# Attention scores of a differential attention layer: one fp32 matmul per score block becomes three fp32r matmuls of rounded parts and rests over 64 rows, with the buffers of the stage laid out anew

## What is computed

```
q = rms_norm((rms_norm(x, ln_g) @ q_w).reshape(b, s, 8, 2, 64), q_norm_g)     # two halves of 64 per head
k = rms_norm(kv[..., :K_DIM].reshape(b, s, 8, 2, 64), k_norm_g)
logits = einsum('bqhcd,bkhcd->bhcqk', qblk, k) * scale + bias               # one per half c, over 64 numbers
p = softmax(where(dist >= 0, logits, -inf))
attn = p[:, :, 0] - lam * p[:, :, 1]
o = rms_norm(einsum('bhqk,bkhd->bqhd', attn, v), subln_g) * (1.0 - lam_init)
mix = o.reshape(b, s, V_TOTAL) @ out_w
```

## Time and profile before

| | |
|---|---|
| median of 3 runs | 2407.59 us (2406.8 to 2408.47) |
| the profiled execution | 2408.69 us, its span 2406.9 us |
| PE / DVE / ACT / POOL busy | 2378.8 / 1408.0 / 1052.7 / 369.7 us |
| differential attention heads, 787 to 985 us of the span | 198 us: PE 194.99, DVE 146.98, ACT 142.42, POOL 18.17 us busy |
| granted TensorE clock | 0.998 of full speed |

### The profile page before, as it was taken

How to read it: one execution, slowest core, us unless ns; L and a number is a source line. 1 busy time by engine, 2 the same in 40 slices (tenths; PEclk the granted TensorE clock), 3 DMA queues, 4 the chain that set the end, 5 groups by cost and what they waited for, 6 DMA issues and landing times.

```text
span 2406.9 us, 29799 instructions
## 1 busy us (share of the span) xinstructions
PE 2378.8 (99%) x11622; PEld 1933.8 (80%) x11622; DVE 1408.0 (59%) x2204; ACT 1052.7 (44%) x1805; POOL 369.7 (15%) x296
## 2 busy tenths in 40 slices
PE   8999999999999999999999999999999999999998
PEld 6677778888888877788888877787788887888887
DVE  6878776763666778766456557534565445443342
ACT  6654554442444677644234334324443334322223
POOL 0352252210111001121012100001211001110101
PEclk9999999999999999999999999999999999999999
DMA  4542223223223221232332332231243322223322
GB/s 164 105 97 79 79 66 101 97 86 107 97 82 119 80 71 52 72 105 92 99 101 89 99 130 71 79 101 62 66 131 128 113 97 88 89 94 103 101 82 85
DMA packets 74269, 226.21 MB, mean 94 GB/s; under 512 B 8080, under 2 KB 12304, under 8 KB 74000
## 3 DMA queue, kind: packets, MB, share of 16 engines
q1 hardware_dynamic: 69696, 215.90, 27.7%
q10 hardware_dynamic: 4432, 8.39, 2.0%
HBM read 215.87 MB, written 8.39 MB: 93 GB/s over the span
## 4 chain that ended last, share of the span: by engine, by line
PE 61%; DVE 1%; issue 0%; ACT 0%; POOL 0%; POOLq 0%; DVEq 0%
PE bank L1162 60%; PE bank L1166 1%; DVE t L2030 0%; DVE t L2027 0%; DVE t L2038 0%; ACT t L1562 0%; DVE t L2034 0%; POOL t L2597 0%; ACT t L1565 0%; POOLq L2816 0%; DVE t L2520 0%; DVEq L2816 0%; DVE t L2366 0%; DVE t L2526 0%; DVEq L771 0%
## 5 line engine op out<-in xcount | busy, mean ns | idle before, releaser
L1162 PE MATMUL bank<-t 128*128 128x512 f32 (+6 forms) x11196 | 2354.7, 376 | 18.4 <-DVE t L2030 8.7
L1162 PEld LDWEIGHTS bank<-t 128*128 128x128 f32 (+2 forms) x11196 | 1890.6, 185 | 451.5 <-issue 80.1
L1562 ACT ACTIVATE t<-t 128x1024 fp32r<-128x1024 f32 (+6 forms) x633 | 539.1, 862 | 636.7 <-PE bank L1162 275.3
L2027 DVE TENSOR_TENSOR t<-t 128x1024 fp32r<-128x1024 f32 (+6 forms) x686 | 625.7, 922 | 260.8 <-ACT t L1562 254.7
L1565 ACT ACTIVATE t<-t 128x512 f32<-128x512 f32 (+6 forms) x609 | 367.1, 617 | 460.5 <-DVE t L2027 304.0
L2597 POOL TENSOR_TENSOR t<-t 128x512 f32<-128x512 f32 (+4 forms) x216 | 328.9, 1528 | 1547.5 <-ACT t L1565 558.9
L2027 DVE TENSOR_TENSOR t<-bank,t 128x512 f32<-128x512 f32 (+4 forms) x411 | 276.1, 676 | 454.7 <-PE bank L1162 444.3
L2030 DVE SCALAR_TENSOR_TENSOR t<-t 128x512 f32<-128x512 f32 (+5 forms) x496 | 367.9, 751 | 103.2 <-ACT t L1565 63.0
L1562 ACT ACTIVATE t<-bank 128x512 f32<-128x512 f32 (+4 forms) x151 | 72.2, 498 | 167.1 <-PE bank L1166 145.2
L2600 POOL TENSOR_SCALAR t<-t 128x128 f32<-128x128 f32 (+3 forms) x64 | 40.1, 633 | 477.9 <-ACT t L1562 246.1
L2030 DVE SCALAR_TENSOR_TENSOR t<-bank,t 128x512 f32<-128x512 f32 x56 | 38.5, 688 | 68.9 <-PE bank L1162 68.9
(11 more groups left out here) (29 smaller groups left out, 42.9 us busy)
## 6 DMA issues: line engine op xcount, KB each, us to landing
t<-in_w SPq DMA_DIRECT2D x304, 512.0 KB, 3.3
t<-in_w SPq DMA_DIRECT2D x48, 384.0 KB, 3.0
t<-in_w SPq DMA_DIRECT2D x56, 320.0 KB, 2.9
t<-in_w SPq DMA_DIRECT2D x28, 256.0 KB, 2.7
tab<-t ACTq DMA_DIRECT2D x1, 2560.0 KB
t<-in_x SPq DMA_DIRECT2D x8, 256.0 KB, 5.8
t<-tab SPq DMA_DIRECT2D x8, 256.0 KB, 3.6
spill<-t ACTq DMA_DIRECT2D x1, 2048.0 KB, 8.3
```

The lines of the kernel that those rows point to most:

```text
L1162: return eng.matmul(out, lhs, rhs, start=start, stop=stop, skip_group_check=loose)
L1562: return eng.activation(out, in_, ACT.Copy, scale=scale)
L2027: return eng.tensor_tensor(out, a, b, o)
```

## The change

Scores are made of three fp32r products over 64 rows, for both halves at once: both banks are taken first, then lo times hi for the halves 0 and 1, hi times lo for both, hi times hi for both. For that, q and k get rounded parts (16 copies on ACT at hsum+3) and rests (16 subtractions on POOL at hsum+4, in place of the fp32 numbers). A head starts five ticks after the `hsum` of its q and k, not three. The squares of the norms are rounded into the places of the rounded parts instead of `hsh`. The second half's exponentials have three rows of their own (`Le`), the first half's five (`Ld`). The o row is written where its rest will lie (`olf`), so the ACT copy out of the bank no longer waits for an older row. The evacuation of q now waits, as that of k did, for the scores of head h-3.

```diff
         def normed(key):
-            return self.past("hsum", key, 3)
+            return self.past("hsum", key, 5)
...
         def q(h):
+            if h >= 3:
+                self.until(lambda: self.past("head", h - 3, 3), ("q", h))
             self.feat(("q", h), "q_w", h * P, "nq", DC, norm="nq")
...
-        self.Qf, self.V = sb(st, [P, 8, S]), sb(st, [P, 8, S])
-        self.kp = [sb(st, [P, S]) for _ in range(3)]
+        self.V = sb(st, [P, 8, S])
+        with ExitStack() as plain:
+            self.olf = sb(plain, [P, 8, S])
+            self.kp = [sb(plain, [P, S]) for _ in range(3)]
+        self.olr = sb(st, [P, 8, S], R)
+        self.kl = [sb(st, [P, S], R) for _ in range(3)]
+        self.kh, self.qh = ([sb(st, [P, S], R) for _ in range(3)] for _ in range(2))
         self.tb = [sb(st, [P, S]) for _ in range(2)]
-        self.Ld = [sb(st, [P, S]) for _ in range(10)]
-        self.Od = [sb(st, [P, S]) for _ in range(2)]
+        self.Ld = [sb(st, [P, S]) for _ in range(5)]
+        self.Le = [sb(st, [P, S]) for _ in range(3)]
         self.rq = [sb(st, [P, S]) for _ in range(2)]
-        self.hsh = [sb(st, [P, S], R) for _ in range(3)]
...
-                w.wait_ge(*sig["hn"].at("q", h))
-                w.wait_ge(*sig["hn"].at("k", h))
-                for c in range(2):
-                    bank = take(("qk", h, i, c))
-                    rows = slice(64 * c, 64 * c + 64)
-                    mm(bank[:, 0:n], buf.Qf[rows, h, i * P:i * P + P], buf.kp[h % 3][rows, 0:n]).then_inc(
-                        *fill(("qk", h, i, c)))
+                (qh, ql), (kh, kl) = buf.operand("q", h), buf.operand("k", h)
+                a = slice(i * P, i * P + P)
+                w.wait_ge(*sig["lo_p"].at("q", h))
+                w.wait_ge(*sig["lo_p"].at("k", h))
+                banks = [take(("qk", h, i, c)) for c in range(2)]
+                halves = (slice(0, 64), slice(64, P))
+                for c, rows in enumerate(halves):
+                    mm(banks[c][:, 0:n], ql[rows, a], kh[rows, 0:n], stop=False)
+                for c, rows in enumerate(halves):
+                    mm(banks[c][:, 0:n], qh[rows, a], kl[rows, 0:n], start=False, stop=False)
+                for c, rows in enumerate(halves):
+                    mm(banks[c][:, 0:n], qh[rows, a], kh[rows, 0:n], start=False).then_inc(*fill(("qk", h, i, c)))
...
-            if h >= 2:
-                w.wait_ge(*sig["lo"].at("o", h - 2))
-            copy(buf.Od[h % 2][:, :], K.of(("ob", h))[:, :]).then_inc(*leave(("ob", h)))
+            copy(K.head_dst(("o", h)), K.of(("ob", h))[:, :]).then_inc(*leave(("ob", h)))
...
         for key in at("hsum", T - 3):
+            if key[0] != "o":
+                w.wait_ge(*sig["hn"].at(*key))
+                copy(buf.operand(*key)[0], K.head_dst(key)).then_inc(*sig["hi"].up(*key))
...
                 for c in range(2):
-                    L = buf.Ld[2 * (b % 5) + c]
+                    L = buf.Le[b % 3] if c else buf.Ld[b % 5]
                     w.wait_ge(*full(("qk", h, i, c)))
+                    if b >= 3 and c:
+                        w.wait_ge(*sig["comb"].at((b - 3) // 4, (b - 3) % 4))
...
+        for key in at("hsum", T - 4):
+            if key[0] != "o":
+                hi, lo = buf.operand(*key)
+                w.wait_ge(*sig["hi"].at(*key))
+                tt(lo, K.head_dst(key), hi.bitcast(F), SUB).then_inc(*sig["lo_p"].up(*key))
```

More of the change, by code:

```diff
@@ L1120, in head_squares @@
         if key[0] == "o":
-            return self.buf.acc, self.buf.hsh[2], self.buf.accr
+            return self.buf.acc, self.buf.operand(*key)[0], self.buf.accr
         n = self.hn_n(key) % 2
-        return self.buf.sqs[n], self.buf.hsh[n], self.buf.sqr[n]
+        return self.buf.sqs[n], self.buf.operand(*key)[0], self.buf.sqr[n]
     def head_row(self, key):
@@ L1135, in head_dst @@
         kind, h = key
-        return self.buf.Qf[:, h, :] if kind == "q" else self.buf.kp[h % 3][:, :]
+        if kind == "k":
+            return self.buf.kp[h % 3][:, :]
+        return self.buf.olf[:, 5 + (h + 1) % 3 if kind == "q" else h, :]
     def av_done(self, stage, a, i, last):
@@ L1837, in diff @@
                 w.wait_ge(*sig["hn"].at("o", h))
-                copy(hi, buf.Od[h % 2][:, :]).then_inc(*sig["hi"].up("o", h))
+                copy(hi, K.head_dst(("o", h))).then_inc(*sig["hi"].up("o", h))
     def mix(T):
@@ L2091, in evacuate @@
                 scaled(g, buf.fv[n % 6][:, :])
-        elif kind == "q":
-            scaled(g, buf.Qf[:, g.key[1], :])
-        elif kind == "k":
+        elif kind in ("q", "k"):
             h = g.key[1]
@@ L2097, in evacuate @@
                 w.wait_ge(*full(("qk", h - 3, NT - 1, 1)))
-            scaled(g, buf.kp[h % 3][:, :])
+            scaled(g, K.head_dst(g.key))
         elif kind == "fg":
@@ L2330, in diff @@
             row, rr = K.head_row(key)[:, :], K.head_squares(key)[0][:, :]
-            dst = buf.Od[key[1] % 2][:, :] if key[0] == "o" else K.head_dst(key)
+            dst = K.head_dst(key)
             gain = {"o": buf.sbl[:, 0:1], "q": buf.qscale[:, :], "k": pc("kn")}[key[0]]
@@ L2375, in diff @@
             if key[0] == "o":
-                two_parts("o", key[1], buf.Od[key[1] % 2][:, :]).then_inc(*sig["lo"].up(*key))
+                two_parts("o", key[1], K.head_dst(key)).then_inc(*sig["lo"].up(*key))
     def mix(T):
```

18 lines of the change are left out of this document (11 added, 7 removed).

## The result

The changed kernel takes **2418.98 us** (median of 6 runs, 2417.87 to 2422.36) against 2407.4 for the kernel before on the same chip: ratio 1.0049, 95% interval 1.0039 to 1.0059. It is slower by 11.6 us; 2407.5 was forecast, with a range of 2404 to 2413.

A forecast was written before the change was run, and what follows sets the result against it. PE, busy 99% of the span, was taken as the bound. Terms -2.8 (groups), +1.0 (head 0), +0.4, +0.5, +0.5 (paired norms), +0.3 (gain not kept) sum to -0.1 us: 2407.5 us, range 2404.0 to 2413.0.

The forecast's parts named there:

- Group cost: PE's score groups in eight heads: three fp32r steps replace one fp32 matmul per half, forecast 2.8 us faster.
- my two ends: Gain of the score groups on PE: 3.5 us at the good end, 2.2 with 13 ns on each step.
- Rival 1: Score matmuls of 128 columns run at the fp32 rate, 844 ns a group, 2410.5 us in all; chance 0.13.
- Rival 2: A half's next weights cannot load while its matmul runs: 2412.8 us; chance 0.07.
- Rival 3: The two halves of a score group do not run together in fp32r: 2418.8 us; chance 0.05.
- Head 0: First score group of head 0: PE waits 1.5 to 1.6 us instead of 0.6 for POOL's subtractions, 1.0 us more.
- Paired norms: Moved o norms meet q norms on DVE, delaying score banks: 0.4 us in head 5, 0.5 each in heads 3 and 7.
- the credited 1.18 us of head 5: PE's longest wait before the change, behind block 3 of head 5, 1.18 us, was expected to mostly go.
- Rival 4: Paired norms show their extra 2.1 us in full to PE in heads 3, 5 and 7: 2412.4 us; chance 0.08.
- POOL's subtractions: 16 subtractions, 23 us on POOL with 18 us of work in the stretch, taken as costing nothing beyond head 0.
- buffers, q's wait, ACT's copies: Three rows of `Le`, q's wait for head h-3, places of squares and the ACT copy no longer waiting: no cost.
- If the total of waits grows by more than 5 us I am wrong: Test set for PE's waits where the heads run: about 5 us expected in all, against 2.6 before.

The follow-up runs named there:

- e11: Changed kernel with each score group's matmuls reordered, all three products of half 0, then all three of half 1: 2419.22 us.
- e13: Kernel before, heads in place, only the norms of the output rows of heads 0 to 5 two ticks later: 2415.12 us.
- e7: Kernel before with one number changed, a head starts 5 ticks after its sums of squares, not 3: 2417.44 us.
- e3: Kernel before with 16 POOL subtractions of 128x512 added on a scratch row, result unused: 2410.89 us.
- e4: Changed kernel with POOL's subtractions cut to 8 of 512 columns, all three products using the rounded parts: 2415.28 us.
- e12: Changed kernel with new scores in heads 6 and 7 only; heads 0 to 5 use one fp32 product on old ticks, new buffers kept: 2406.68 us.
- e15: Changed kernel with the norm of o1 alone two ticks later, away from that of k3: 2416.19 us.
- e8: Changed kernel with heads back on the old ticks (3, not 5) and the rests made by DVE instead of POOL: 2424.29 us.

## Why the prediction was wrong

Its answer to "how long does PE take for a group" was nearly right; that to "when is DVE late" was not, by 11 us.

- *Group cost, -2.8 us:* measured -2.2, which is the lower of my two ends (the 13 ns on each step); the middle was 0.6 too good. A step at 128 keys takes the 0.11 us that I took. Rival 1 (128 columns at the fp32 rate, 0.84 us a group) is refuted by 0.48. Rival 2 (weights can't load under their own half) is refuted by six loads in 0.53 us. Rival 3 (halves not together) is refuted too, by 0.89 us for a 512-key group, where its 0.205 us plus 6 cycles a column give 1.49, and by e11 for the halves written one behind the other, though its price, 2418.8, lies closest to the result: the right number by the wrong mechanism.
- *Head 0, +1.0:* right. PE waits 1.49 us for POOL at 799.12, forecast 1.5 to 1.6, 0.59 before.
- *Paired norms, +1.4:* **this step failed.** The mechanism is the right one, its list and its price were not. I looked at one consumer of DVE, the score banks in heads 3, 5 and 7, and credited the waits that the move takes away. At those three 512-key groups the waits are 0.68, 0.47 and 0.17 us, where the kernel before hid 0.47 in heads 5 and 7, and the credited 1.18 us of head 5 did go. With 0.52 at head 5's 384-key group that is some 0.9 us: in its own places the forecast was not too low. It left out the 384-key groups of heads 1, 2 and 4 (0.46 to 0.52 us each) and above all the other consumer, the sums of squares on PE: 2.52 us for q3 (o1 with k3), 0.99 at 930.68 (o3 with q5) and 1.25 at 948.94 (o4 with q6). The meetings alone cost 5.5 us of the stage (e13; 3.8 at full clock), and the dearest in the changed kernel, o1 with k3, was on no list of mine, neither in the account of the change nor in the sum; behind its 2.5 us the clock fell. Rival 4 had the form (2.1 us in full at each of three places), but at the score banks of heads 3, 5 and 7.
- *The move of the heads themselves* had no term at all beyond that. With it the late heads cost 10.3 us of the stage (e7), 4.8 more than the meetings alone; 2.0 us of that, at heads 1 and 6, are the evacuation ahead of the `add_min`, and 1.8 the two waits behind ACT copies. No run separates these.
- *"At nothing": POOL's subtractions.* The second step that failed. I asked whether POOL had room for 23 us and did not ask what DVE does meanwhile. In the kernel before they cost 2.9 us (e3). In the changed one they cost less than the 3.7 us of e4 suggest: of the stage's 4.0 us between the two, 1.5 are head 0's wait, which is on my list, and 1.7 the lower clock behind the 2.5 us wait, which e4's profile doesn't show though it has that wait; 0.8 are left.
- *"At nothing": buffers, q's wait, ACT's copies.* Right as far as e12 shows it, which has four of the sixteen copies. e4 has all of them, and against e7 it gains 2.0 us of the stage (at full clock) where the groups give 2.2.
- *The sum, by runs:* late heads +9.6 (e7), then scores and copies -2.2 (e4 against e7), then the subtractions +3.7 (changed kernel against e4) make 11.1 of the 11.6 measured. In the stage of the profiled executions, with the 1.7 us of lower clock set apart: late heads +8.6, scores and copies -2.0, subtractions with head 0's wait +2.3, lower clock +1.7, together the 10.7 measured (281.3, 279.3 and 281.6 us for e7, e4 and the changed kernel at full clock). The differences of two medians are good to about 2 us.
- *"If the total of waits grows by more than 5 us I am wrong"*: it grew by 12.2, some 1.9 of which had been hidden inside four groups before.

## What to carry to other kernels

Where one engine is in order and has no pause, as DVE had (15.00 of 15.5 us), moving a unit of work is not free because it is the same work: list for each moved operation what now stands behind it in its queue, and every consumer of that, not the one consumer that waits today. Before work is given to an idle GpSimd, look which DVE instructions of two SBUF operands run beside it; here 23 us of work on an idle engine cost 10 us of DVE (1419.3 us against 1408.9 in e4). And a gain of 0.1% on the bounding engine is worth taking only where nothing must be moved for it, as in heads 6 and 7, where it then was too small to measure.

## What I had not expected of the hardware

- A blocked DVE instruction shows as a long one, with no idle time for the block: 1.76 us for 0.72 (the 0.59 us ahead of it are a wait for the result of POOL's scaling). In a table of groups only the mean tells (725 to 799 ns, 1220 to 1457).
- Two halves of the array take their fp32r products side by side even if the program writes all three of one half first (e11, 0.53 us for six loads in both orders). And a half's next weights load while its own matmul runs: the third loads at 810.36, as the second matmuls begin at 810.35 and the third at 810.58.
- A wait of PE can cost more than its length: 2.5 us, then 1.7 us more at the lower clock. The clock also fell behind waits of 2.0 us (e13) and 1.5 us (e15). But e4 has the same wait of 2.5 us and a clock of 1.00 in 866 to 872 us, and the changed kernel the same one of 1.5 us at full clock, so it doesn't always follow. The lower clock at 1415 to 1425 us (0.83) shows in the changed kernel, e11, e13 and e15, and of the others only in e8 (0.58 in 1424 to 1428 us, the same place of its program, since its stage ends 5 us later), though this part of the program is the same in all. What decides it stays open.
